# One 512-column product for both activation parts in the ungated feed-forward phases

## The reference

```
x = x + jnp.square(jax.nn.relu(h @ ffn_w1[l])) @ ffn_w2[l]        # 2048 -> 8192 -> 2048
...
val, gate = jnp.split(h @ w_up[i], 2, axis=-1)                     # 2048 -> 2 x 5632
gate = causal_depthwise_conv_2(gate, conv_w[i], conv_b[i])
x = x + (val * jax.nn.gelu(gate, approximate=False)) @ w_down[i]   # 5632 -> 2048
```

## Time and profile before

| | |
|---|---|
| runs | 2881.17, 2884.65, 2885.1 us; median 2884.65 us |
| profiled execution | span 2882.9 us; no other time of its own is given |
| TensorE busy (matmuls) | 2802.8 us, 24650 matmuls |
| VectorE busy | 1823.4 us |
| ScalarE busy | 1245.7 us |
| GpSimd busy | 396.0 us |
| read from memory | 503.12 MB, 177 GB/s over the span |
| chain that ended last | PE 64%, of it lines 670, 671 and 672 with 21% each |
| granted TensorE clock | 0.990 of full speed |

### The profile page before, as it was taken

How to read it: one execution, slowest core, us unless ns; L and a number is a source line. 1 busy time by engine, 2 the same in 40 slices (tenths; PEclk the granted TensorE clock), 3 DMA queues, 4 the chain that set the end, 5 groups by cost and what they waited for, 6 DMA issues and landing times.

```text
span 2882.9 us, 61146 instructions
## 1 busy us (share of the span) xinstructions
PE 2802.8 (97%) x24650; PEld 2752.2 (95%) x24650; DVE 1823.4 (63%) x2175; ACT 1245.7 (43%) x1511; POOL 396.0 (14%) x549
## 2 busy tenths in 40 slices
PE   8999699999999999999999999999999999999998
PEld 8999687999989999999999999998999999999998
DVE  6678747775435655655555668697667655665664
ACT  5355223544334543444434545434454443443444
POOL 0000230110002139300461210000110000010011
PEclk9999899999999999999999999999999999999999
DMA  6654002566635566666667565554555665556564
GB/s 235 195 192 147 16 31 88 191 189 204 190 102 164 190 197 190 219 213 189 197 194 236 191 195 163 193 196 157 193 192 189 197 192 193 193 188 199 184 198 149
DMA packets 138418, 514.10 MB, mean 178 GB/s; under 512 B 15360, under 2 KB 15616, under 8 KB 136960
## 3 DMA queue, kind: packets, MB, share of 16 engines
q1 hardware_dynamic: 138240, 511.58, 54.9%
HBM read 503.12 MB, written 8.40 MB: 177 GB/s over the span
## 4 chain that ended last, share of the span: by engine, by line
PE 64%; DVE 4%; issue 1%; ACT 1%; DVEq 0%; ACTq 0%
PE acc L670 21%; PE acc L671 21%; PE acc L672 21%; DVE lo L473 1%; PE work L2170 0%; ACT hi L379 0%; DVE s_xr L2514 0%; PE acc L2203 0%; DVE tb L543 0%; DVE sq L2523 0%; DVE ua L2514 0%; DVE ub L2514 0%; DVE s_xr L2505 0%; DVE sq L2503 0%; DVE ta L2522 0%
## 5 line engine op out<-in xcount | busy, mean ns | idle before, releaser
L670 PE MATMUL acc<-a,hi 128*128 128x256 f32 x5504 | 1527.0, 277 | 16.3 <-DVE lo L473 14.5
L671 PE MATMUL acc<-a,hi 128*128 128x256 f32 x5504 | 1521.5, 276 | 0.0
L672 PE MATMUL acc<-a,lo 128*128 128x256 f32 x5504 | 1521.4, 276 | 0.0
L473 DVE TENSOR_TENSOR lo<-qx,hi 128x1024 fp32r<-128x1024 f32 x704 | 896.4, 1290 | 674.6 <-ACT hi L379 672.9
L670 PEld LDWEIGHTS acc<-a,hi 128*128 128x128 f32 x5504 | 1035.3, 188 | 20.5 <-issue 14.8
L671 PEld LDWEIGHTS acc<-a,hi 128*128 128x128 f32 x5504 | 1035.3, 188 | 0.8 <-issue 0.5
L672 PEld LDWEIGHTS acc<-a,lo 128*128 128x128 f32 x5504 | 1035.3, 188 | 0.0
L379 ACT ACTIVATE hi<-qx 128x1024 fp32r<-128x1024 f32 x704 | 733.9, 1057 | 646.4 <-PE acc L672 629.0
L620 POOL TENSOR_TENSOR a<-th,a 128x512 f32 (+1 forms) x64 | 84.9, 1327 | 1381.2 <-ACT a L424 1381.1
L473 DVE TENSOR_TENSOR lo_x<-next_raw,hi_x 128x1024 fp32r<-128x1024 f32 x128 | 162.2, 1281 | 115.0 <-ACT hi_x L379 115.0
L670 PE MATMUL acc<-a,hi_in 128*128 128x256 f32 x768 | 215.4, 280 | 9.8 <-DVE lo_in L473 9.8
(11 more groups left out here) (503 smaller groups left out, 2779.2 us busy)
## 6 DMA issues: line engine op xcount, KB each, us to landing
qx<-in_ffn SPq DMA_DIRECT2D x256, 512.0 KB, 4.2
raw_in<-in_w_in SPq DMA_DIRECT2D x96, 512.0 KB, 4.3
qx<-in_w_in SPq DMA_DIRECT2D x92, 512.0 KB, 3.7
qx<-in_up_gate SPq DMA_DIRECT2D x88, 512.0 KB, 4.2
qx<-in_up_val SPq DMA_DIRECT2D x88, 512.0 KB, 4.3
qx<-in_down SPq DMA_DIRECT2D x88, 512.0 KB, 4.2
next_raw<-in_wq SPq DMA_DIRECT2D x32, 512.0 KB, 4.3
next_raw<-in_wk SPq DMA_DIRECT2D x32, 512.0 KB, 4.3
```

The lines of the kernel that those rows point to most:

```text
L473: eng.tensor_tensor(self.lo[:, slot, :], self.raw[:, slot, :], self.hi[:, slot, :].bitcast(F32), ALU.subtract).then_inc(self.s_lo, 1)
L670: eng.matmul(out, self.hi[:, slot, cols], a[:, 0, :], start=opens, stop=False)
L671: eng.matmul(out, self.hi[:, slot, cols], a[:, 1, :], start=False, stop=False)
L672: ins = eng.matmul(out, self.lo[:, slot, cols], a[:, 0, :], start=False, stop=closes)
```

## The change

In the phases `ffn1`, `ffn2`, `val` and `down` (`wide=True`) the products of lines 670 and 671 become one matmul of 512 columns: the high weight block by the high and low activation parts, which lie side by side. It fills a whole PSUM bank, so a unit takes two banks, `acc[:, 2s]` and `acc[:, 2s + 1]`, and each half of it is opened and closed by itself. The product with the low weights stays at 256 columns and is added into the first half of its bank. The sum of the two halves, which the accumulation made for nothing before, is now DVE's: where the unit is added to `x`, two additions take the place of one; where it is multiplied by `rstd`, a `tensor_reduce` over the two halves comes first, and the multiplication follows from SBUF. Phases next to a wide one (`apart=True`) only use banks 0 and 2 in place of 0 and 1. The gate keeps its three matmuls.

```diff
+    def place(self, ph, s):
+        return 2 * s if ph.wide or ph.apart else s
...
     def evacuate(self, eng, ph, v, s):
-        got = self.acc[:, s, :].rearrange("p (t n) -> p t n", t=2)
+        at = self.place(ph, s)
+        if ph.wide:
+            got, rest = (self.acc[:, at:at + 2, h * T:(h + 1) * T] for h in range(2))
+        else:
+            got = self.acc[:, at, :].rearrange("p (t n) -> p t n", t=2)
...
+            if ph.wide:
+                link(eng.tensor_tensor(xp, rest, xp, ALU.add))
             eng.tensor_tensor(xp, got, xp, ALU.add).then_inc(self.s_free, 1)
...
-        eng.tensor_tensor(cur, got, rs, ALU.mult).then_inc(self.s_free, 1)
-        if kind in ("z", "sigmoid"):
-            return
-        eng.wait_ge(self.s_free, free)
+        if ph.wide:
+            halves = self.acc[:, at:at + 2, :].rearrange("p t (h n) -> p t n h", h=2)
+            eng.tensor_reduce(cur, halves, AX.X, ALU.add).then_inc(self.s_free, 1)
+            eng.wait_ge(self.s_free, free)
+            link(eng.tensor_tensor(cur, cur, rs, ALU.mult))
+        else:
+            eng.tensor_tensor(cur, got, rs, ALU.mult).then_inc(self.s_free, 1)
...
     def unit(self, eng, ph, v, j, beside=None):
-                out = self.acc[:, s, t * T:(t + 1) * T]
+                out = self.acc[:, at + t, :] if ph.wide else self.acc[:, at, t * T:(t + 1) * T]
...
-                    opens, closes = kt == 0 and t == 0, kt == CK * ph.nc - 1 and t == 1
+                    opens, closes = kt == 0 and (t == 0 or ph.wide), kt == CK * ph.nc - 1 and (t == 1 or ph.wide)
...
+                    elif ph.wide:
+                        cols = slice(q * UNIT + t * P, q * UNIT + (t + 1) * P)
+                        eng.matmul(out, self.hi[:, slot, cols], a.rearrange("p h n -> p (h n)"), start=opens, stop=False)
+                        ins = eng.matmul(out[:, 0:T], self.lo[:, slot, cols], a[:, 0, :], start=False, stop=closes)
...
-            up = s.phase("ffn1", ..., after=fo if q == 0 else None, sum_after=q == 0)
+            up = s.phase("ffn1", ..., after=fo if q == 0 else None, sum_after=q == 0, wide=True)
```

More of the change, by code:

```diff
@@ L148 @@
     k: object = None
+    wide: bool = False
+    apart: bool = False
+    links: int = 0
 @dataclass
@@ L281, in phase @@
         ph.k = k
+        ph.links = k.links + ph.wide
         if kind == "emit":
@@ L286, in phase @@
             t["u"] += units
-        for f, a_unit in k.counts().items():
+        for f, a_unit in dict(k.counts(), links=ph.links).items():
             t[f] += units * a_unit
@@ L489, in link @@
             ins.then_inc(self.s_link, 1)
-            eng.wait_ge(self.s_link, v * k.links + (b["links"] + steps[0]))
+            eng.wait_ge(self.s_link, v * ph.links + (b["links"] + steps[0]))
         if kind in ("gained", "acc", "sumsq"):
@@ L542, in evacuate @@
             return
-        eng.tensor_tensor(cur, got, rs, ALU.mult).then_inc(self.s_free, 1)
-        if kind in ("z", "sigmoid"):
-            return
-        eng.wait_ge(self.s_free, free)
+        if ph.wide:
[5 more added lines that the diff above has]
+            eng.tensor_tensor(cur, got, rs, ALU.mult).then_inc(self.s_free, 1)
+            if kind in ("z", "sigmoid"):
+                return
+            eng.wait_ge(self.s_free, free)
         if kind == "rwkv":
@@ L637, in unit @@
         b = ph.base
-        s = (b["u"] + j) % 2
+        at = self.place(ph, (b["u"] + j) % 2)
         if isinstance(v, int) and v == 0 and ph.ready:
@@ L1869, in attentions @@
                 stats = alloc(nc, xs, "stats", [P, 16])
-                fo = s.phase("wo", "wo", 8, 4, 2, a1, "gained", out=s.a0, g="norm_ffn_g")
+                fo = s.phase("wo", "wo", 8, 4, 2, a1, "gained", out=s.a0, g="norm_ffn_g", apart=True)
                 cross_attention(nc, s, qx, kx, vx, pe_, pt, stats, a1, semaphores(nc, xs), fo)
@@ L2560, in feed_forwards @@
             up = s.phase("ffn1", "ffn1", 8, 4, 2, s.a0, "relu2", out=a1, w0=32 * q,
-                         after=fo if q == 0 else None, sum_after=q == 0)
+                         after=fo if q == 0 else None, sum_after=q == 0, wide=True)
             if q < 3:
-                down = s.phase("ffn2", "ffn2", 8, 4, 2, a1, "acc", w0=32 * q, after=up)
+                down = s.phase("ffn2", "ffn2", 8, 4, 2, a1, "acc", w0=32 * q, after=up, wide=True)
             else:
                 down = s.phase("ffn2", "ffn2", 8, 4, 2, a1, "gained", out=s.a0, w0=32 * q, after=up, g=s.gg[:],
-                               gsq="final1_g")
+                               gsq="final1_g", wide=True)
             ffn += [up, down]
@@ L2573, in feed_forwards @@
         pa = s.phase("in_a", "w_in_2", GA2 // 2, 4, 2, s.a0, "bias", out=ua, g="b_in", after=ffn[-1], sum_after=True,
-                     double=norm)
+                     double=norm, apart=True)
         w0, raw = 4 * GA2 // 2, 6
@@ L2587, in feed_forwards @@
         bs = s.phase("br_ssm", "br_ssm", 8, 1, 8, s.a0[:, 4:8], "br_ssm", out=a2, src=ub, g0=KT, after=g2, lead=True)
-        wo = s.phase("w_out_2", "w_out_2", 8, 4, 2, a2, "gained", out=s.a0, g="ffn2_g", after=bs)
+        wo = s.phase("w_out_2", "w_out_2", 8, 4, 2, a2, "gained", out=s.a0, g="ffn2_g", after=bs, apart=True)
         phs = [ba, g1, g2, bb, bs, wo]
@@ L2592, in feed_forwards @@
             gate = s.phase("gate", "up_gate", n // 2, 4, 2, s.a0, "gate", out=ub, g="c2", g0=3 * t0, p0=t0,
-                           taps=3, w0=2 * t0, after=wo if q == 0 else None, sum_after=q == 0)
-            val = s.phase("val", "up_val", n // 2, 4, 2, s.a0, "val", out=a2, src=ub, w0=2 * t0)
+                           taps=3, w0=2 * t0, after=wo if q == 0 else None, sum_after=q == 0, apart=True)
+            val = s.phase("val", "up_val", n // 2, 4, 2, s.a0, "val", out=a2, src=ub, w0=2 * t0, wide=True)
             down = s.phase("down", "down", 8, n // 4, 8 if q == 2 else 2, a2, "sumsq" if q == 2 else "acc",
-                           w0=32 * q, after=val, ends=q == 2)
+                           w0=32 * q, after=val, ends=q == 2, wide=True)
             phs += [gate, val, down]
```

## The result

| | median | runs | over before |
|---|---|---|---|
| before | 2884.88 us | 2881.17 to 2885.29 us | |
| after | 2930.05 us | 2929.46 to 2930.8 us | 1.0159 (95% interval 1.0147 to 1.0172) |

The account below looks back on a forecast made before the run. TensorE's matmul distances, set by weight loads at 113.3 ns, were taken as the bound in the feed-forwards. The span went 2882.9 - 38.4 + 0.95 + 0.70 = 2846.2, the median to 2848.0 us; range 2843 to 2865.

Parts of the forecast that it names:

- the reading of 113.3: TensorE in the feed-forwards: one weight load sets the 113.3 ns between 256-column matmuls, whose own 109 lies under it.
- rival 2: TensorE: most of the 6.6 ns is a slower stream, 2877.7 us; with all of it, 2886; chance 0.09, halved between them.
- The 64-column matmuls: Evidence from the trace: eight 64-column matmuls with full 128 x 128 loads, 111.4 ns from load to load, read as load-bound.
- The 215.3 of plain float32: Evidence from the trace: float32 matmuls of 256 columns start 215.3 ns apart, the basis for pricing the 512-column matmul at 215.6.
- The upper bound of the 512 columns: TensorE, the pair's 512-column matmul: at most two matmuls of today, 226.6 ns, where nothing is gained.
- 113.3 for the short matmul: TensorE, the pair's 256-column matmul: stays at 113.3 ns; at 118 it would cost 16 us of the gain.
- the rivals on TensorE: Other accounts of the matmul distances, with times of 2863.3, 2877.7 or 2886, 2833 and some 3590 us.
- The count: TensorE in both feed-forwards: 3456 triples become pairs, some 3456 fewer matmuls and loads, 11.1 ns less each, 38.4 us less.
- VectorE: Evacuations: 54 reductions of some 1.14 us and 56 further additions, busy time up 100 us, mostly where VectorE has room.
- The end: Program's end: the last unit's addition of 0.70 us stands in the chain twice, +0.70 us.
- unit 2: First `ffn1`, where the norm's root delays the evacuation: 0.56 us to spare against 1.15 + 0.36, so +0.95 us, once.
- Rival 4: TensorE: a 512-column fp32r matmul streams at plain float32's pace, the pair 543 ns, some 3590 us; chance 0.04.

Follow-up runs that it names:

- experiment 3: TensorE alone, no kernel: single fp32r matmuls beside weight blocks of 32, 64 and 128 columns; with 32, 256 columns still take 113 ns, 128 columns 60.
- experiment 6: TensorE alone: series of 40 in fp32r and bfloat16, then 356 series of pairs or triples in mixed order; fp32r 256 columns 113.3 ns at best, equal places differ.
- experiment 9: Changed kernel with low weights 64 bytes later in wide phases, first `ffn1` phase kept in triples: 2885.26 us, ratio 1.0002 to before.
- experiment 2: TensorE alone, operands' starting bytes varied: at low 352 a pair takes 351 ns and a triple 340, at 416 340 and 352.
- experiment 4: Kernel before with its low weights' buffer 64 bytes later, all three matmuls kept: 2976.81 us, ratio 1.0313 to before.
- Experiment 8: Changed kernel with pairs in `val` and `down` only, at the original places: 2904.93 us, ratio 1.0072 to before.
- experiment 5: Changed kernel with low weights 64 bytes later in the wide phases only: 2907.19 us, ratio 1.0085 to before.
- experiment 7: Changed kernel with low weights 48 bytes later in the wide phases only: 2906.23 us, ratio 1.0081 to before; its runs lie in two groups.
- experiment 1: Changed kernel with the 512-column matmul cut into two of 256, banks, reduction and second additions kept: 2885.78 us, ratio 1.0005 to before.

## Why the prediction was wrong

**The step that failed** is the reading of 113.3: "I read 113.3 as one weight load, which starts when a matmul starts and must be over before the next can; the matmul's own 106.7 + 2 = 109 lies under it." Shown instead, by experiments 3 and 6: the fp32r stream itself takes 113.3 ns for 256 columns, under a load of 32 columns too, and for 512 it takes 226.6 at the least (230 or more under the small load), where I had put 215.6. The load (111.8) lies under the stream, by a hair. That is rival 2 in its full form ("with all 6.6 in the stream nothing at all, 2886"), to which I gave half of 0.09; experiment 9 has its time, 2885.3. With this reading put right the pair costs 340.0 at best in place of 328.9, and the gain is gone: 11.1 of the 24.5 ns by which the pair was over the forecast.

Two rows misled me. The 64-column matmuls show a load bound, and it is real, but 111.4 isn't 113.3: the 2 ns between them belonged to something else. The 215.3 of plain float32 was the nearest row for "a long matmul over a load", yet of a format that needs twice the time for a column. It says that a hidden load costs nothing there; it says nothing of how fast fp32r streams. No row of the trace had an fp32r matmul without a load of full width, so nothing there could separate the two. The Trainium skill's formula of N/2.4 + 2.5 ns ("TensorE: Matmul & The Clock Gate", section "Back-to-back issue gap") gives 109.2 and 215.8: the bfloat16 series agree to the tenth, the fp32r ones don't.

**The upper bound of the 512 columns was wrong as well.** I wrote "above, two matmuls of today, 226.6, where nothing is gained". It took 233.4 at the kernel's places. And "I keep 113.3 for the short matmul; with 118 it would cost 4.7 x 3456 = 16 us of the gain" named the effect with the wrong size: it took 120.0. Together they make 13.4 ns a pair over the triple, the 46 us, and the other part of the 24.5. None of the rivals on TensorE had a time between 2886 and 3590. Experiments 2 and 4 show that this depends on the places: 64 bytes turn it about for both forms. Experiment 8 shows that it goes with the number of pairs. Experiments 5, 6, 7 and 9 show that it also depends on what ran before: with the same places, 350 or 340.

**What held.** The count: 3456 triples, matmuls down by 3456. VectorE: the reduction took 1.218 us for 1.14, busy time rose by 103.4 us for 100, and it delays nothing (experiment 1). The end: one more row of 0.70. At unit 2, 0.95 us of waiting was forecast and 0.2 measured: the unit had become 32 x 13.4 = 0.43 us longer, where I had counted 0.36 shorter, and 0.95 - 0.79 is the 0.2 (in experiment 7, with pairs at 340 and so neither term, it is 0.60). Rival 4 ended on the right side for a wrong reason: 512 fp32r columns don't run at the pace of plain float32, 543 ns a pair.

**What stays open.** Why fp32r needs 113.3 ns for 256 columns, and what in the meeting of weight reads and activation reads sets 340, 347, 350 or 353, is only argued. That both are read from the same memory, at addresses whose distance counts, suggests that the reads get in each other's way in a fixed pattern; no run looked inside. What in a disturbance changes the pace is open too: line 721 did it in experiment 5 and not in 7, the wait in 7, where the pace in 5 had already changed. Nor was it tried whether a pair thrown out of pace could be brought back by something cheaper than a phase of triples.

## What to carry to other kernels

When every matmul costs its columns and a remainder, don't give the remainder to the load before a run with a narrow weight block has said so, in the same number format. If the stream owns it, merging two matmuls that share weights wins nothing, however many instructions it saves. And before such a change is judged, measure the operand places: in this kernel, bound by fp32r matmuls, 64 bytes in the distance between weights and activations are worth 4% of a triple (340 against 353 ns), and a well tuned place is tuned for one form of the sequence only.

## What the hardware showed beyond the expected

- fp32r streams 256 columns in 113.3 ns at best and 512 in 226.6, bfloat16 in 109.2 and 215.8, all at a granted clock of 1.00. At all places that were tried, a triple of 256-column matmuls and a pair of 512 + 256 have the same floor, 340.0 ns.
- The distance of the weight block from the activations, by its remainder to 256 bytes, moves a pair between 340 and 355 ns and a triple between 340 and 372. 64 bytes are 93 us of this kernel.
- The same instructions at the same places have more than one steady pace (340, 347, 350, 353 ns). It changed at four records of plain float32 matmuls in one kernel and at a wait of 0.60 us in another, and then stayed for hundreds of microseconds.
